# Two-layer streaming encoder on one core: the table that places expert steps between trunk instructions

## The reference

```python
q = (xb @ w_q).reshape(PEER_BLOCK, PEER_HEADS, 2, PEER_QDIM // 2)
s = jnp.einsum('thpd,hpnd->thpn', q, sub_keys)
s1, i1 = lax.top_k(s[:, :, 0], PEER_TOPK)
s2, i2 = lax.top_k(s[:, :, 1], PEER_TOPK)
cand = (s1[..., :, None] + s2[..., None, :]).reshape(...)
top_s, pos = lax.top_k(cand, PEER_TOPK)
e_idx = jnp.take_along_axis(cand_idx, pos, axis=-1)
gate = jax.nn.softmax(top_s, axis=-1)
act = jax.nn.gelu(jnp.einsum('thkd,td->thk', u[e_idx], xb), approximate=False)
return jnp.einsum('thk,thkd->td', gate * act, v[e_idx])
```

## Time and profile before

| | us |
|---|---|
| median of 3 runs | 4274.04 (4265.19 to 4279.12) |
| profiled execution | 4273.03 |
| its span, first to last instruction | 4271.2 |

### The profile page before, as it was taken

How to read it: one execution, slowest core, us unless ns; L and a number is a source line. 1 busy time by engine, 2 the same in 40 slices (tenths; PEclk the granted TensorE clock), 3 DMA queues, 4 the chain that set the end, 5 groups by cost and what they waited for, 6 DMA issues and landing times.

```text
span 4271.2 us, 64529 instructions
## 1 busy us (share of the span) xinstructions
PE 3205.0 (75%) x22584; PEld 1964.3 (46%) x22584; DVE 2479.4 (58%) x6208; ACT 1665.8 (39%) x4730; POOL 1135.3 (27%) x1028
## 2 busy tenths in 40 slices
PE   7788986478888986858988887467988985445444
PEld 4576773145545673424545575134554673111111
DVE  2322219977556617687645627978646717865544
ACT  2213113364465313343465423364466323333333
POOL 0000002344333001234433301434433101443332
PEclk8779997578888997758898998578898997555555
DMA  7302337999999438999999945999999634999997
GB/s 252 106 22 94 108 114 310 393 378 401 391 377 395 190 115 305 345 359 391 401 402 387 408 172 224 384 400 392 400 385 378 273 114 182 391 407 421 421 420 312
DMA packets 247588, 1315.65 MB, mean 308 GB/s; under 512 B 21216, under 2 KB 35168, under 8 KB 116192
## 3 DMA queue, kind: packets, MB, share of 16 engines
q0 software_dynamic: 147456, 1073.81, 62.1%
q1 hardware_dynamic: 99808, 237.72, 15.7%
HBM read 1309.34 MB, written 2.10 MB: 307 GB/s over the span
## 4 chain that ended last, share of the span: by engine, by line
PE 28%; DMA 24%; DVE 19%; PEld 8%; ACT 8%; issue 7%; DVEq 2%; ACTq 2%; PEldq 2%; POOL 0%; POOLq 0%; SPq 0%
DMA row<-uv,e_idx 19%; DVE row L1526 7%; PE bank L617 5%; PE bank L671 5%; PEld bank L657 3%; PE bank L1002 3%; DMA weights<-w_in 2%; DMA weights<-w_ada 2%; PEld bank L671 2%; DVE reg L1424 2%; PEld bank L934 2%; PE bank L657 1%; DVE reg L1419 1%; PE bank L850 1%; ACT e_diag L1098 1%
## 5 line engine op out<-in xcount | busy, mean ns | idle before, releaser
L1941 POOL DMA_INDIRECT row<-uv,e_idx x1024 | 1135.1, 1109 | 3099.1 <-PE bank L617 1739.8
L1526 DVE CUSTOM_DVE_ANT_0 row<-row,e_rep 128x1024 f32<-128x1024 f32 x1024 | 1243.1, 1225 | 677.5 <-DMA row<-uv,e_idx 622.5
L617 PE MATMUL bank<-row,e_diag 128*32 128x256 f32 x8192 | 871.8, 513 | 726.4 <-ACT e_diag L1098 697.9
L617 PEld LDWEIGHTS bank<-row,e_diag 128*32 128x32 f32 x8192 | 195.2, 125 | 1283.7 <-ACT e_diag L1098 1050.8
L1094 ACT ACTIVATE e_ge<-e_dot 128x1 f32<-128x1 f32 x1024 | 206.5, 202 | 1208.4 <-DVE e_dot L1526 1192.1
L671 PE MATMUL bank<-hT,weights 128*128 128x256 f32 (+2 forms) x2176 | 533.5, 401 | 41.6 <-ACT hT L1163 24.8
L671 PEld LDWEIGHTS bank<-hT,weights 128*128 128x128 f32 (+2 forms) x2176 | 411.2, 194 | 165.5 <-issue 53.9
L657 PE MATMUL bank<-hT,weights 128*128 128x256 f32 x1536 | 365.1, 387 | 14.3 <-issue 12.7
L1098 ACT ACTIVATE e_diag<-mask,e_wg 128x32 f32<-128x32 f32 x1024 | 329.1, 321 | 74.1 <-issue 4.0
L1096 ACT ACTIVATE e_wg<-e_gate,e_ge 128x1 f32<-128x1 f32 x1024 | 301.5, 294 | 74.0 <-issue 4.1
L657 PEld LDWEIGHTS bank<-hT,weights 128*128 128x128 f32 x1536 | 281.0, 190 | 98.1 <-issue 61.9
(11 more groups left out here) (270 smaller groups left out, 3871.3 us busy)
## 6 DMA issues: line engine op xcount, KB each, us to landing
weights<-w_ada SPq DMA_DIRECT2D x48, 1024.0 KB, 7.5
weights<-w_mac SPq DMA_DIRECT2D x64, 768.0 KB, 8.5
weights<-w_in SPq DMA_DIRECT2D x44, 1024.0 KB, 10.0
weights<-w_mb SPq DMA_DIRECT2D x32, 768.0 KB, 4.3
weights<-w_out SPq DMA_DIRECT2D x16, 1024.0 KB, 5.0
weights<-w_pq SPq DMA_DIRECT2D x16, 1024.0 KB, 5.0
row<-uv,e_idx POOLq DMA_INDIRECT x1024
weights<-w_in SPq DMA_DIRECT2D x8, 1056.0 KB, 18.2
```

The costliest lines, as they stand in the source:

```text
L617: last = mm(acc_ps[g % 2][c * QT:(c + 1) * QT, 0:2 * P], e_diag[:, n % RING, :], row[n % RING][:, D + c * 2 * P:D + (c + 1) * 2 * P], star ...
L1526: V.tensor_tensor_reduce(row[r][:, 0:D], row[r][:, 0:D], e_rep[g % 2], 1.0, 0.0, ALU.mult, ALU.add, e_dot[:, r:r + 1]).then_inc(dots, 1)
L1941: pool.indirect_dma_start(row[r], None, uv, bass.IndirectOffsetOnAxis(ap=e_idx[:, j:j + 1], axis=0)).then_inc(rows_landed[r], 16)
```

## The change

The nine strings of `STEPS` are replaced: three laps for each of three engines. No other line differs. The numbers of places and of steps are those of before (the digits of a string add up to all steps, or to one or two fewer, which `turns.rest()` emits). The strings of laps 1 and 3, equal in the old table, differ in a few digits in the new one on each engine. The diff, without the third string of each engine:

```diff
@@ -255,44 +255,44 @@
 DIGITS = "0123456789abcdefghijklmnopqrstuvwxyzABCDEFGHIJKLMNOPQRSTUVWXYZ"
 STEPS = {
     "PE": (
-        "100000000000011101030s00C001120203011110111110000010010080011100103001000100200100010001000211000011000001000100001000"
-        "0001001000000100100110001000100010110000100100100010000100000030001001000002101100020010001010100001001100001010001000"
-        "0001000010000010001011001000000100010010000110000000100301100020122112000100000000110100311011111001000120014012200001"
-        "0200000100004010100000010000001213011001101001011310111101110111101110110111101110110111100000000000000000000000000000"
-        "00000000000000000000000000000000000000000000000000000000000000000000000000000000000000000000000000000000000000",
-        "10000000000001001011000001000000020011100020110110001000010000200000111010011001011010101000100220001100000010000000y0"
-        "0121100120010001001000000100010001011000100010010001000010000001000100000100010110001000100010130000101000200100000100"
-        "0001000210000010001011000100010001011000010010010001000010000001000010000010001011000100010030001001000002000000110010"
-        "0300100012111110000001000011000221011111201200002021310110000200000000002040001000000001000012130101310001211121101111"
-        "1011101101111011101111031011111110100010000000100000010022000010010001002000010101001110111000000000000000000000000000"
-        "00000000000000000000000000000000000000000000000000",
...
+        "1000000010020100020010010010010020001111101111110000220390000000r00001000002100000210000020000000000002001001100000000"
+        "0000003000010100020110000001000001010000000000000001000000000000011000001000101101010010001001100000000000000020000001"
+        "0010000120000010011021001000000100000010000010000000100100100100111111100001000000000002210131102011000010042011300000"
+        "0100000000003011100000000000000000000100001302000031013011021101101101101101101110110110110113001000012000000200401000"
+        "00012100000000302100020200101011011012111010101001001300000000010100100101001004000000000010100100101200000001",
+        "1000000030001300011000002000000000000610000000000000112110000000000003010110001002202021000000040400010010000000000120"
+        "0011209000010011001000400100000200110000010000000000200000000001001000010100110100010001000001010000000000000001000000"
+        "0000000110000010001011010100100011301000010000000001000000000101000010000010003011000100010000001001000001000000010010"
+        "0110000102111101000000000000000241013110201100001002210110200100000000000030111000010000000000000000010006121101211010"
+        "0101010101010101010101010010101010102000101010100000110210000000020000000000000205000100110110111011011011011011002111"
+        "10001110111000010002031111103010101012100000000000",
...
     ),
     "ACT": (
-        "200000000010AD00001000110023002020010004010010001001312504223510202101111203112041012212041130201021112210221010100017"
-        "1010111324110120420120300140021010121300100010000010101010432030202020302020203020201000000000000000000000000000000000"
-        "00000000000000000000000000000000000000000000000000000000000000",
-        "200220100000001002035000100011000020013010100010401000010061100011pe02312401202010211206012031103112031120201021133120"
-        "2110300010041110110415212010612010200220120010121300010001202114304020202030203010304030203002101020100201000101001000"
-        "111101201000000000000000000000000000000000000000000000000000000000",
...
+        "200000100021003000001000112000100030210300201102030027t001333100301202310111001011102212020021211131121110110010100005"
+        "0110000417011001710110201000231000000000001000000000001122042040203020202020203010301040040205000005000000010221002210"
+        "10202030302020201004010000030100001100000006000000020100000000",
+        "303340100000000201043000101001000000005010001010801000000161210010f001351400102211210111001011102212060010201132112110"
+        "1100200000051010000527011001511010210000231010000000000001000163304010301020202020201020101003000400000200000000110000"
+        "051100202020202020202007000100040100011100000007101310140000000000",
...
     ),
     "DVE": (
-        "1000KJ0010010202311010001000130101001200100110010011110011010013101101001011101001001020012102100100110101000101011014"
-        "10311000101101010010101101200310102011501010b1010100910012071202001100810100010000010001000114001301110011001100120011"
-        "0011001100120011001100110010001000000000000000000000000000000000000000000000000000000000000",
-        "13500000230503000013103100300100003104003010035000001000A0000011310011010011001101001011010100101011012003100100110101"
-        "0003011101030031001001101010001010110120031003021150000101a0001100c100110702020110107101100000010070030030020020120020"
-        "02002012002002014011003002010000100001001102101a010000000000000000000000000000000",
...
+        "1021301050001020300011221122212122121220001000000100z00000000103002003000200000000200010104102010000100000000100010103"
+        "0041000011000000001000211041030010101030100090000000e00110070301000000600000000000001000011011011103010011001101100110"
+        "011001100110011010110011001100110111012000101111011101111d020303020202010310031002061110000",
+        "9521000030150301010020000000800010110900000118110200000000000100i00000000103030102000200100000100020004102010000100000"
+        "000100010103004100002111000000100021003103010101014000000090000000f000100703010000006000000021010040020120020010110110"
+        "0200200200200101100100200100100000011003010101180202020202020206010410120e3010000",
...
     ),
 }
 
```

More of the change, by code:

```diff
@@ new lines @@
+        "0101010101010101010101010010101010102000101010100000110210000000020000000000000205000100110110111011011011011011002111"
+        "10001110111000010002031111103010101012100000000000",
+        "1000100000200100110010010010010001010022101111000110220390000000r00001000002100000210000010000000000001111001000000001"
+        "0000003000100100010110001000001000110000000000000001000000000000011000001000101101010010001001100000000000000020000001"
+        "0010000120000010011021001000000100000010000010000000100100100100111111100001000000000002210131102011000010042011300000"
@@ new lines @@
+        "303340100000000201043000101001000000005010001010801000000161210010f001351400102211210111001011102212060010201132112110"
+        "1100200000051010000527011001511010210000231010000000000001000163304010301020202020201020101003000400000200000000110000"
+        "051100202020202020202007000100040100011100000007101310140000000000",
+        "201000000021003000102000001000100013030201201102030027t001332100213102211102001011102212020021211131121110110010100005"
+        "0110000417011001710110201000321000000000001000000000001122042040203020202020203010301040040205000005000000010221002210"
@@ L285 @@
+        "10202030302020201004010000030100001100000006000000020010000000",
     ),
     "DVE": (
[L287 to L290 removed]
@@ L296 @@
+        "1111301050101010100121221122212122121220001000000100z00000000103002002100100000000200111004003000001100000000100010103"
+        "0041000011000000001000211041030010101030100090000000e00110070301000000600000000000001000011011011103010011001101100110"
+        "011001100110011010110011001100110111012000101111011101111d020303020202010310031002061110000",
     ),
```

11 lines of the change are left out of this document (removed).

## The result

The kernel with the new table takes **4138.9 us** (median of 4 runs, 4127.78 to 4146.67) against 4269.61 for the kernel before in the same comparison: a ratio of 0.9688, 95% interval 0.9663 to 0.9713, or 131 us. The profiled executions took 4127.78 and 4273.03 us, 145 apart. The forecast was 4211, a gain of 62. The direction was right and 4139 lies inside the stated 4110 to 4310, but the gain was half of what came.

A forecast was written before the change was run, and what follows sets the result against it. DVE was taken to bound the head of laps 1 and 3, PE (0.9 us a row) or the transfers (2.6 to 2.7) the stages behind; -26, -26 and -10 make -62 us, from 4273 to 4211, range 4110 to 4310.

The forecast's parts named there:

- the head: Start of each lap up to rwkv: 34 fewer rows give -59 us in laps 1 and 3; lap 2 -20.
- the attention: Attention stage of laps 1 and 3: 24 rows added at the pace of the transfers, +22 us a lap.
- merge b: Merge of branch b after the attention: 17 rows added at 0.93 us each, +16 us in laps 1 and 3.
- the output stage: Output and PEER queries at the lap's end: 19 rows added at 0.93 us, +18 us; lap 2, 31 rows, +29.
- the hand-over: Lap's end: the last unit's sum and write into x now delay the next lap's first squares, +4 us a lap.
- The slower rival: In the output stage, rows ahead of the residual add stall DVE and PE; late rows cost 2.0 us, total 4339, chance 0.14.
- the gain handed back: Rows in merge b and output cost 1.27 us each, heads reach only 235 us: total 4282, chance 0.17.
- the table in vain: Rows pile up before rwkv because gathers wait for routing; head stays at 279 us, total 4329, chance 0.03.
- dividing the difference by the rows gives what one row costs its stage: Stage time with rows minus lap 0's, per row: lap 1 rwkv 0.87 us, projections 1.27, merge 0.94.
- rwkv: The rwkv blocks of laps 1 and 3: 71 to 54 rows at 0.87 us each, -15 us a lap; lap 2 -10.
- the projections: GLA and DSA projections of laps 1 and 3: 58 to 47 rows at 1.27 us each, -14 us; lap 2 -18.
- better than the sum: DVE waits less for rows: projections cost 0.93 us a row, head comes to 205 us; total 4136, chance 0.23.

The follow-up runs named there:

- after: The kernel with the new step table, against the kernel before with the old one: 4138.9 us, ratio 0.9688.
- the short dot: The kernel before with each row's dot product over 256 of 1024 columns: 4192.24 us with whole rows, 3755.1 us with half the bytes.

## Why the prediction was off

**Right.** The views and the stages; the head (-59 against -66 in lap 1; -20 against -29 in lap 2), set by DVE's work and by the two batches; the attention at the pace of the transfers (+22 against +28); merge b (+16 against +15), at 0.9 us a row as read from the merge; the output stage, 18 us for 19 rows against 21 in lap 3 (in lap 2, with the hand-over, 33 against 43, so 10 too little); the hand-over, 4 us against the 4 between the output stages of laps 1 and 3. The slower rival (a late row costs 2.0 us) is excluded: late rows cost 0.9 to 1.4. So is the gain handed back, which had heads of 235 us where 213 were measured, and the table in vain, which had 279.

**Wrong: the price of a removed row.** The step that failed is "dividing the difference by the rows gives what one row costs its stage". (190-128)/71 = 0.87 is the mean over all rows of the stage. It was multiplied with the 17 rows that leave, as if each cost the same. The runs show another price for the last rows: 33 us for the 17 that left in after, 1.9 each, and 43 us for 17 put back, 2.5 each, against 0.4 each between 20 and 54 rows. The rows that leave are the dear ones. The mis-sized terms are rwkv (-15, measured -33) and the projections (-14, -26), together -51 instead of -29 in lap 3 and -43 instead of -28 in lap 2: 30, 22 and 15, or 67 us over the three laps. With the 5 us of lap 2's merge they are 72 of the missing 83 us between the profiled executions (145 less 62). Against the medians (131 less 62) 69 us are missing.

The figures for a second bound were there. The working itself says that rwkv took 2.7 us a row at a DMA share of 1.00. Taking the pace of the transfers for each row would have given 17 x 2.6 = 44 us as the upper bound; 33 were measured, and 43 for the rows put back. Instead the working used the mean as the only value and gave rwkv no bounds at all. The bound would have been right for a reason that fails, since the 33 us stay with half the bytes. The second case, "better than the sum", had the right total (4136), and that was partly luck. Its projections came nearly out (-30 against -26 in lap 1), but it had the head at 205 where 213 were measured, and left rwkv at -15 where -33 came. It named the chain between the engines as an argument against rwkv.

**Why a removed row gives so much is open.** The transfers, which the working named as the limit of those stages, do not explain it: with half the bytes the tables still differ by 144 us. One reading is two limits. In rwkv the transfers (2.6 us a row) and the chain DVE-ACT-PE, lengthened by each row's dot (the part of the sums was not separated), stand near each other, so that a row removed relieves both, while half the bytes alone gave 31 us over three laps, the short dot alone 1, and both 95. That these two together set the price of a row in after was argued, not tried. What makes the last rows of the projections dear was not settled: half the bytes gave 5 us there, the short dot with it 5 more, narrow sums 4, more buffers none.

**The clock.** The other reading, which does not exclude the first, is the granted clock. That of rwkv rose from 0.83 to 0.91 (0.76 with the rows put back) and that of the projections from 0.86 to 0.92. An estimate of its part, from length times clock: rwkv of lap 1 fell from 158 to 143 and the projections from 157 to 144. At the new clocks these are 16 and 14 us, close to the 15 and 14 of the forecast; the other 17 and 12 us would be the clock's. In lap 2's rwkv, where the clock did not move, the rows were worth more than forecast all the same (16 to 19 us against 10). What moved the clock was not shown. The second case named its rise from the Trainium skill (TensorE: Matmul & The Clock Gate, What's actually happening), which has activity release the slow level, but gave it no price; the run with narrow sums fits that page, since less work came with 0.68 instead of 0.81. The limit of about 358 GB/s for one core (the Trainium skill, DMA: Bandwidth & Descriptors, Specifications), weighed beside the sum, did not show: merge and merge b ran at 419 and 417 GB/s. The same page (Bandwidth) has about 425 GB/s as measured with the pair's other core idle, and no stage here went above that.

## What to carry to other kernels

Price a step that is moved by what the stage gives back for the last ones of its kind, not by the mean: here the last 17 rows of rwkv were worth 1.9 to 2.5 us each, where the mean was 0.87. Two points of the same stage (a stage with the work and one without) only give the mean; a third count gives the slope, and until there is one the pace of the busiest resource may stand as the other end of the range. A DMA share of 1.00 does not say that fewer bytes help: look at whether a chain of about the same length stands behind it. Before a difference between two stages is put on the work, look at the granted clock of both and at a stage in which nothing was changed; here such a stage moved by up to 10 us between traces. And try a new order before trusting a price: three rows more in a full stage came with 15 us more.

## What the runs showed of the hardware

- Gathers of half rows (4 KB per partition instead of 8) ran the last experts at 562 us instead of 709, 243 GB/s instead of 382, with six buffers, and at 505 us and 271 GB/s with twelve. With six buffers half the bytes took 79% of the time.
- Less work on TensorE came with a lower clock: with row sums a quarter as wide, rwkv went from 0.81 to 0.68 and PE's busy time from 169.60 to 166.11 us only.
- The same stage with the same instructions (rwkv of lap 0, no gathers) took 127 to 137 us in twelve traces. The granted clock went from 0.77 to 0.71 with it, and length times clock stayed at 96 to 98.
- In the output stage of after, blocks of weights that share the engines with gathers stand on the chain (w_out 15.0%):

```profile
by line: DMA weights<-w_out 15.0%; PE bank L671 14.9%; PE bank L1002 12.9%; DVE reg L1424 6.8%; DVE reg L1419 4.7%; PE bank L617 4.1%; PE bank L1021 3.7%; PE bank L987 3.6%; DVE reg L1429 3.4%; DVE row L1526 3.3%; DMA weights<-w_small 3.0%;
```
